# Second-half projections in pieces between first-half attention steps, and input factors on POOL

## What is computed

```python
h = rms_norm(h_res, pre_mix_g[l])
proj = jnp.einsum('bld,dc->blc', h, w_in[l])
q1, q2, k1, k2, v, u = jnp.split(proj, [...], axis=-1)
q1 = pad(partial_rope(heads(q1, QK_DIM), cos, sin))      # the same for q2, k1, k2
o = diff_attention(q1, q2, k1, k2, vh, lam)              # softmax(q1 k1) - lam softmax(q2 k2), causal, times v
y = s5_ssm(u.reshape(...), a_re[l], a_im[l], ...)        # a linear state space model (SSM) along the sequence
y = jax.nn.gelu(y, approximate=False)
y = y * jax.nn.sigmoid(jnp.einsum('blc,cd->bld', y, w_glu[l]) + b_glu[l])
mix = jnp.einsum('blc,cd->bld', jnp.concatenate([o, rms_norm(y, ...)], axis=-1), w_out[l])
```

## Time and profile before

| | us |
|---|---|
| runs | 3842.01, 3850.78, 3851.14 (median 3850.78) |
| profiled execution | 3846.03, of which the span from first to last instruction 3844.2 |
| mean granted TensorE clock | 0.897 of full speed |
| busy in the span: PE, DVE, ACT, POOL | 3300.6, 1812.4, 925.8, 1884.1 |

### The profile page before, as it was taken

One profiled execution on the slowest core, in us unless ns is written; L12 is line 12 of the kernel. 1 busy time (PEld: TensorE's weight loads), 2 busy tenths in 40 slices (PEclk: granted clock), 3 DMA queues, 4 the chain that ended last, 5 costly groups with the idle time before them and its releaser, 6 DMA issues.

```text
span 3844.2 us, 48841 instructions
## 1 busy us (share of the span) xinstructions
PE 3300.6 (86%) x19888; PEld 2560.0 (67%) x19888; DVE 1812.4 (47%) x2626; ACT 925.8 (24%) x1625; POOL 1884.1 (49%) x1004
## 2 busy tenths in 40 slices
PE   5886388668999876997999998898899999989997
PEld 4654266356777654676777776676677777778785
DVE  6377411234344255266655655247655556322233
ACT  3000011233333223213223332412223323210012
POOL 3131000033555545574656665565566655567773
PEclk9998555588999988999999998999999999999998
DMA  3511211131122223332222214232222222322221
GB/s 127 107 61 58 76 43 32 25 121 50 66 94 71 71 84 126 138 112 72 80 72 64 83 64 148 95 132 85 72 75 78 74 75 69 121 82 94 93 99 61
DMA packets 140576, 321.89 MB, mean 84 GB/s; under 512 B 25040, under 2 KB 62096, under 8 KB 140224
## 3 DMA queue, kind: packets, MB, share of 16 engines
q1 hardware_dynamic: 57024, 207.64, 16.2%
q10 hardware_dynamic: 83328, 111.12, 9.3%
HBM read 275.58 MB, written 43.12 MB: 83 GB/s over the span
## 4 chain that ended last, share of the span: by engine, by line
PE 72%; DVE 18%; ACT 4%; ACTq 2%; DMA 2%; issue 2%; POOL 0%; DVEq 0%; POOLq 0%
PE ps L1563 27%; PE ps L1604 11%; PE ps L1592 11%; PE ps L1794 3%; PE ps L1332 2%; PE ps L1429 2%; PE ps L1413 2%; DVE acc_dense L1968 1%; DVE cab L1968 1%; DVE act_lo L1968 1%; DVE ffh_lo L2581 1%; PE ps L1457 1%; PE ps L1342 1%; DVE wv L1968 1%; PE ps L1409 1%
## 5 line engine op out<-in xcount | busy, mean ns | idle before, releaser
L496 POOL TENSOR_TENSOR w_hi<-w_raw,ones 128x1024 fp32r<-128x1024 f32 x396 | 780.7, 1972 | 1694.8 <-DMA w_raw<-weights 1680.9
L498 POOL TENSOR_TENSOR w_lo<-w_raw,w_hi 128x1024 fp32r<-128x1024 f32 x396 | 976.3, 2465 | 31.0
L1563 PE MATMUL ps<-act_hi,w_hi 128*128 128x512 f32 x1632 | 677.8, 415 | 6.6 <-DVE act_lo L1968 6.6
L1563 PE MATMUL ps<-act_lo,w_hi 128*128 128x512 f32 x1632 | 654.8, 401 | 0.0
L1563 PE MATMUL ps<-act_hi,w_lo 128*128 128x512 f32 x1632 | 650.4, 399 | 0.0
L1563 PEld LDWEIGHTS ps<-act_hi,w_hi 128*128 128x128 f32 x1632 | 313.8, 192 | 96.1 <-issue 15.5
L1563 PEld LDWEIGHTS ps<-act_hi,w_lo 128*128 128x128 f32 x1632 | 312.6, 192 | 72.7
L1563 PEld LDWEIGHTS ps<-act_lo,w_hi 128*128 128x128 f32 x1632 | 313.2, 192 | 66.0 <-issue 1.7
L1968 DVE TENSOR_TENSOR acc_dense<-acc_dense,ps 128x512 f32<-128x512 f32 x352 | 242.2, 688 | 234.2 <-PE ps L1592 174.7
L1592 PE MATMUL ps<-w_hi,ffh_hi 128*128 128x512 f32 x704 | 294.9, 419 | 58.2 <-DVE acc_dense L1968 54.5
L580 ACT ACT_TABLE_LOAD x204 | 261.7, 1283 | 295.6 <-PE ps L1563 107.2
(11 more groups left out here) (360 smaller groups left out, 5057.3 us busy)
## 6 DMA issues: line engine op xcount, KB each, us to landing
w_raw<-weights SPq DMA_DIRECT2D x396, 512.0 KB, 3.3
rw<-rw_t ACTq DMA_DIRECT2D x24, 256.0 KB, 2.3
rw<-lora_t ACTq DMA_DIRECT2D x24, 256.0 KB, 2.0
ca_scratch<-ca ACTq DMA_DIRECT2D x8, 544.0 KB, 3.0
ca<-ca_scratch ACTq DMA_DIRECT2D x8, 544.0 KB, 3.9
row<-x ACTq DMA_DIRECT2D x8, 512.0 KB, 3.4
m_t<-kd_scratch ACTq DMA_DIRECT2D x64, 64.0 KB, 3.4
row_dense<-x ACTq DMA_DIRECT2D x8, 512.0 KB, 3.8
```

The costliest lines, as they stand in the source:

```text
L496: pool.tensor_tensor(w_hi[:, s], raw, ones[:, 0:1].to_broadcast([P, 1024]), MUL).then_inc(w_hi_made, 1)
L498: pool.tensor_tensor(w_lo[:, s], raw, w_hi[:, s].bitcast(F32), SUB).then_inc(w_ready, 1)
L1563: mm = pe.matmul(out, ws[w][:, s, P * k:P * k + P], acts[a][:, k, x], start=(k, w, a) == (0, 0, 0), stop=(k, w, a) == (KT - 1, 1, 0))
```

## The change

1. *The second half's queries, keys and values leave `project`.* `PROJ` keeps u (all), the value tiles of the first half and the learned tokens, and of queries and keys the spans of the first half and the learned tokens: 29 steps instead of 41. The twelve others form `FAR`: four value tiles, then eight tiles of queries and keys, each in four pieces of six matmuls (`project_far`), 49 steps with the last rotation. Their weight units come a second time in `ORDER`, 12 more units.
2. *`HEAD_EVENTS` is built anew:* the first attention step, three far pieces, then a piece after about three of four attention steps; the eight scan parts after every second attention step from the start, and from the 24th on an output block after every sixth. `PROJ_EVENTS` holds no scan part any more. The scan ends one step earlier, since the last state is not used.
3. *The input factors `g_t` are computed on POOL* (`input_factors`, six operations a batch on 128x512 elements, each waited for), with a weight unit split after each batch.
4. *Buffers.* `row`, `xn`, `rope`, `qk_raw`, `qk_o` and others move; `rope` and `qk_o` hold 528 columns, and the rotary table of the second half is loaded later; `v_o`, `yb`, `ca2` and `m_t` have one buffer instead of two; the scan's scratch `wx` and `a16` have places of their own. Second-half attention waits for the later stores.

```diff
-    spans_of = lambda m: 2 + (m >= 4)
-    PROJ = ([("u", m, s) for m in range(4) for s in range(3)] + [("v", i, 0) for i in range(NT + 1)]
-            + [("qk", m, s) for m in range(8) for s in range(spans_of(m))])
+    spans_of = lambda m: (0, 2) if m >= 4 else (0,)
+    PROJ = ([("u", m, s) for m in range(4) for s in range(3)] + [("v", i, 0) for i in (*range(HALF), NT)]
+            + [("qk", m, s) for m in range(8) for s in spans_of(m)])
+    FAR = [("v", i) for i in range(HALF, NT)] + [("qk", m) for m in range(8)]
...
-    PROJ_EVENTS = (["proj", "ssm"] + ["proj"] * 14 + ["ssm", "proj", "ssm", "proj", "proj"] * TB + ["ssm", "proj"] * 5)
+    PROJ_EVENTS = ["proj", "ssm"] + ["proj"] * 14 + ["ssm", "proj", "ssm", "proj"] * TB
...
+    def head_events():
+        events, done = ["heads"] + ["far"] * 3, 3
+        extra = ([["ssm"]] + [[]]) * (SCAN_PARTS + 1) + ([[]] * 5 + [["ssm"]]) * TB
+        for n in range(ATT_STEPS - 1):
+            now = min(4 * len(FAR) + 1, 3 + (4 * len(FAR) - 2) * (n + 1) // (ATT_STEPS - 5))
+            events += ["heads"] + ["far"] * (now - done) + (extra[n] if n < len(extra) else [])
+            done = now
...
-    ORDER = [(0, u) for u in range(U_OUT)]
+    ORDER = [(0, u) for u in range(U_GLU)] + [(1, u) for u in range(U_V, U_GLU)] + [(0, U_GLU), (0, U_GLU + 1)]
...
+        def input_factors(b):
+            q = slice(TQ * b, TQ * b + TQ)
+            if b:
+                pool.wait_ge(g_turned, TQ * b)
...
+            mul(first, back(0), inp(0))
+            mul(second, back(1), inp(1))
+            mul(g_t[:, 0], first, second, op=SUB)
+            mul(first, back(0), inp(1))
+            mul(second, back(1), inp(0))
+            mul(g_t[:, 1], first, second, g_ready, b + 1, ADD)
...
+        split_to(8)
+        pool.wait_ge(factors_ready, 1)
+        for b in range(TB):
+            input_factors(b)
+            split_to(10 + b)
...
+        def project_far():          # on TensorE
+            pe.wait_ge(proj_kept, len(PROJ))
+            pe.wait_ge(rope_done, ROPES)
+            for n, (kind, m) in enumerate(FAR):
+                for part in range(4):
+                    if kind == "v":
...
+                        far_values(m, part)
+                    else:
+                        if part == 0:
+                            pe.wait_ge(proj_kept, len(PROJ) + n)
+                        dense_products(AT[1, U_QK + m], ps[:, 0, :], part, half_cols(1), 3)
+                        if m and part == 1:
+                            rotate_far(m - 1)
+                    yield
...
         def build_factors(b):
...
-            back = lambda ri: pw[:, ri, q, 0:STEP][:, :, ::-1].unsqueeze(3).to_broadcast([P, TQ, STEP, SG])
-            inp = lambda ri: bb[:, ri, q, :].unsqueeze(2).to_broadcast([P, TQ, STEP, SG])
-            tmp = cab[:, :, 0:TQ * STEP * SG].rearrange("p a (q l h) -> p a q l h", q=TQ, l=STEP)
-            cmul(g_t[:, 0], g_t[:, 1], back(0), back(1), inp(0), inp(1), tmp[:, 0], tmp[:, 1], last=g_ready)
```

More of the change, by code:

```diff
@@ L167, in proj_done, with far_done @@
         return proj_psum, sum(not ends_unit(*p) for p in PROJ[:n + 1])
+    PROJ_COUNT = sum(not ends_unit(*p) for p in PROJ)
+    def far_done(n):
+        kind, m = FAR[n]
+        if kind == "v" and m < NT - 1:
+            return proj_psum, PROJ_COUNT + n + 1
+        return unit_done, AT[1, U_V + 3 if kind == "v" else U_QK + m] + 1
     def rope_index(m, s):
-        return 2 * m + max(0, m - 4) + s
+        return m + max(0, m - 4) + s // 2
     TB, TG, TQ = 8, 4, 2
@@ L671, in project @@
                     give(fn(qk_raw[:, m % 2, c0:c1], src, ACT.Copy, scale=QK ** -0.5 if m < 4 else 1.0), proj_kept)
-                    if m >= 2 and s == 1:
+                    if m >= 2 and s == 0:
                         store_turned(m - 2)
                 yield
[L675 to L678, removed]
+            store_turned(6)
+            yield
+            yield
             store_turned(7)
@@ L763, in attention @@
                 act.wait_ge(glu_lo, 4)
+                for r in range(2):
+                    act.wait_ge(qk_stored[r], 16 * 8)
                 load_queries_and_keys(1, 0)
@@ L1272, in _ @@
         heads = attention(0)
+        far = project_far()
         for side in HEAD_EVENTS:
-            next(heads if side == "heads" else states)
+            next({"heads": heads, "ssm": states, "far": far}[side])
+        for _ in far:
+            pass
         for _ in glu(0):
@@ L2207, in ssm @@
                 yield
-            now, other = wv[:, 0:2, :], wv[:, 2:4, :]
+            now, other = wx[:, 0:2, :], wx[:, 2:4, :]
             for part in range(SCAN_PARTS):
-                for c in range(1 + SCAN_RUN * part, 1 + SCAN_RUN * (part + 1)):
+                for c in range(1 + SCAN_RUN * part, min(1 + SCAN_RUN * (part + 1), NSTEP - 1)):
                     tt(now, xs[:, :, :, c], a16[:, 0], MUL)
```

179 lines of the change are left out of this document (125 added, 54 removed).

## The result

The changed kernel takes 3815.3 us (median of five runs, 3803.9 to 3828.6) against 3842.0 for the kernel before on the same chip; the ratio is 0.992, 95% interval 0.990 to 0.994. So it is faster, by 27 us (by the interval 23 to 38) and by less than 1%, where 80 were forecast: the sign was right, the size about a third. The five runs of the kernel before include two under the three that the prediction knew, so its median here is 3842.0 and not 3850.8. The profiled execution of the changed kernel took 3815.3 us (span 3813.3) against 3846.0 (span 3844.2): 31 us less.

What follows compares the result with a forecast made beforehand. TensorE was taken as the bound, at half clock from 447.5 to 731 us. First scores at 329, plus 80 and 242, end at 651, 80 us early: 3846.0 becomes 3766 (about 3766 to 3771), range 3705 to 3865.

Steps and rivals of the forecast that it cites:

- Part 1: Projections before attention: batch 7's factor products at 298 us instead of 329, first scores at 329, 88 us earlier.
- The cycle of 23 us: Projections: one batch takes 23 us instead of 27.2, two VectorE stretches beside POOL included; bounds 20 and 33.
- Rival (c): Projections: POOL's factor operations hinder VectorE's, batches take up to 33 us; 40 us lost, 3806 us; chance 0.13.
- Part 2: The scan, with four attention units and fifteen far pieces beside it, takes 80 us and ends at 409.
- Part 3: Rest of first-half attention with outputs and far pieces, from 409: 242 us, ending at 651, 80 us early.
- The idle term: Stretch from 409 to 651: 25 us of TensorE idle time, against 47 in the stretch before the change.
- the 3.5 us of raising: Stretch from 409: half clock for 3.5 us at each of eight output blocks until it rises again, 28 us.
- Rival (b): From 409 to 740: pieces don't lift the clock, 3855 to 3878 us, 3860 taken; chance 0.17.

Runs made afterwards that it cites:

- E11: E1 with GpSimd waiting in every batch until that batch's output factors are made before it splits its weight unit: 3752.6 us, ratio 0.975 to the kernel before.
- E4: The changed kernel with the pieces of the second half's projections spread over the first 18 attention steps rather than nearly all: 3867.1 us, ratio 1.004 to the kernel before.
- E7: The changed kernel with all pieces beside the scan, six for each eighth, no attention between them: 3848.0 us, ratio 1.001 to the kernel before.
- E9: The changed kernel with one matmul of each output half, 320 of the 448 output matmuls left out: 3745.3 us, ratio 0.974 to the kernel before.
- E3: The changed kernel with the input factors back on VectorE, the moved projections kept: 3833.9 us, ratio 0.996 to the kernel before.
- E5: The kernel before with only its outputs cut into quarters, one after each of four attention steps of six: 3824.4 us, ratio 0.994.
- E1: The changed kernel with each first-half output block cut into quarters, one after each of four attention steps of six: 3773.3 us, ratio 0.981 to the kernel before.
- E2: The changed kernel with GpSimd waiting for the last batch of output factors before splitting the weight units that follow: 3813.2 us, ratio 0.991 to the kernel before.
- E6: The changed kernel with one of three passes of every product in the second half's projections, 2 matmuls a piece: 3814.1 us, ratio 0.992 to the kernel before.

## Why the prediction was right in sign and wrong in size

- **Part 1 was right in its mechanism, and its number in part by luck.** Batch 7 at 298, measured 300.1; first scores 329, measured 324.0. The cycle of 23 us came out as 23.3, but made of 21.3 for the first five and 33.5 for the last, in which POOL goes on to split the units behind it without a pause; the forecast had no such batch. In the others POOL's split stretches VectorE twice, as priced (0.69 to 2.27 and 1.49 to 3.50 us; VectorE, then POOL):

```profile
212.81 2.27 DVE L2084 TENSOR_TENSOR qk_o<-qk_o,rope_sin_part 128x512 f32<-128x512 f32 x1
215.11 3.50 DVE L2084 TENSOR_TENSOR cab<-pw,c_t 128x544 f32<-128x544 f32 x2
...
212.15 2.37 POOL L522 TENSOR_TENSOR w_hi<-w_raw,ones 128x1024 fp32r<-128x1024 f32 x1
214.60 2.67 POOL L524 TENSOR_TENSOR w_lo<-w_raw,w_hi 128x1024 fp32r<-128x1024 f32 x1
```

  E11 shows that they lie on the chain: without them a batch takes 18.5. It is the split that does it: GpSimd's factor operations (1.07 and 1.29 us, forecast 1.2 to 1.6) hardly meet VectorE's chain; in the batch of E11 they stand beside its copies out of PSUM. Rival (c) had the mechanism and missed the size, except in the last batch.
- **Part 2 was near, with two errors against each other.** Scan to 409, measured 413.0; from first scores on it took 89 us instead of 80, and first scores came 5 us early. That the pieces beside it cost nothing held too, but the reason I gave (TensorE has room) is half of it. The other half is that POOL stays off the scan (two operations). E4 and E7 show what happens otherwise: 42 to 44 us. I had looked for POOL's hold on VectorE in the projections only.
- **Part 3 failed.** The step is "I take the attention with its pieces at full, the outputs midway (88), and for each of eight blocks 3.5 us at half clock until it rises again (28)". The stretch took 279 us plus the 7.5 behind the last turn, where 242 was forecast, and began 5 us late. By terms: pieces 69 for 47 (+22), outputs 97 for 88 (+9), attention 69 for 46 + 28 (-5), rotations 10 for 8 (+2), idle with the tail 41 for 25 (+16). That is +44, and with the late start -80 becomes -31. The largest term is the pieces at full clock. The idle term is the second: of the 33 us in front of the last turn 24.6 are the wait for the normed attention output, which was 29.0 before, so the pieces hardly filled it.
- **What the term missed.** I took the clock as something that is raised once behind each output block and then stays. The trace shows it change level 22 times, 42% full in all. More than a third of the pieces' own matmuls (76 of 210, half of the pieces' time) run at half clock, at 0.45 us where the others take 0.26: the 3.5 us of raising were charged to the rest, but the pieces pay too. E9 shows that it isn't the outputs alone that drop it, so "eight times" had no ground. That attention came out near its 74 us (69) is luck: it was to be at full but for 28 us, and over half of its time (38 us) is at half.
- **Rival (b), slower,** had its turning point at a tenth of the stretch at full; 42% is past it. Of what it described, half clock for all attention and outputs, E7 is the nearest case that ran (its pieces beside the scan): 3848.0, level with the kernel before.
- **The attribution was wrong as well.** I put the gain down to attention and outputs. E3 shows that most of it, 19 us by the medians (of 27) and 24 by the profiled executions (of 31), is the six VectorE operations a batch that went to POOL, the part I had sized at 4.2 us a batch and treated as a detail of the cycle. 8 x 4.2 = 34 us was in my own numbers. This share holds with the projections already moved; by themselves the factors were not tried.
- **Two rules.** That the gate follows busyness (Trainium skill, TensorE: Matmul & The Clock Gate, Part 1) I had set aside for the row at 0.50. The runs bear that out: the changed kernel's stretch is busy 88% of the time at 0.71, the thin one's 86% at 0.55, the one of E5 88% at 0.50. E1 is busy 89% at 0.81. Busy time doesn't order them. The shared SBUF interface (Trainium skill, GPSIMD Engine Reference, Specifications) agrees with E2 and E11. Its price in the projections is 29 us from batch 1 to 7 (140.0 in the changed kernel, 111.2 in E11), and 42 to 44 us more where splits fall on the scan (E4, E7), which rival (c) did not look at.

## What to carry to other kernels

Before work is moved into a stage at half clock to lift it, count on both levels in turns (here 42% full, 62% with the finer mixing of E1): the matmuls that raise the clock are themselves slow. An operation moved to another engine off a per-batch chain can be worth its time in every batch (here 19 to 24 of the 34 us that it took), and an order of GpSimd work against a VectorE chain (E11 over E1, one wait a batch) was worth 21 us, three quarters of the whole change. When a step frees buffers earlier, look at what the freed buffers let start, and beside whom.

## What was not expected of the hardware

- A VectorE operation of 0.21 us that meets a GpSimd operation with two inputs takes up to 2.42 us and ends within 0.1 us of it. One of 0.72 us went on to 290.11, 0.57 behind the end of the split at 289.54. So the stretch is the rest of the GpSimd operation, not a share of the VectorE one. GpSimd is slowed much less: a split takes 2.37 and 2.70 us beside the output factors, 1.89 and 2.36 alone, and 1.90 and 2.40 beside the scan.
- Taking away 141 matmuls of 512 columns made TensorE busy 4 us longer in the stretch they stood in (E6): the granted clock went from 0.71 to 0.55.
- Between 413.7 and 692.4 us the granted clock of the changed kernel changed level 22 times.
